# The values projection of an mLSTM layer as seven block products instead of eight

## The reference, cut to what matters

```python
proj = h @ w_in                                   # h: (tokens, 1024), after rmsnorm
q = proj[..., :HK] ...                            # HK = 4 heads x 128
k = proj[..., HK:2 * HK] ... * (MLSTM_DK ** -0.5)
v = proj[..., 2 * HK:2 * HK + HV]                 # HV = 4 heads x 256 = 1024 columns
o = proj[..., 2 * HK + HV:2 * HK + 2 * HV]        # output gate
```

## Time and profile before

| what | value |
|---|---|
| median of the timed executions | 1197.86 us (1196.89 to 1198.4, 3 runs) |
| the profiled execution, its own time | 1195.74 us |
| its span, first to last instruction | 1193.9 us |
| granted TensorE clock over the span | 0.999 of full |
| PE, DVE, ACT busy over the span | 99%, 72%, 51% |
| DMA | 148.60 MB, mean 124 GB/s |

### The profile page before, as it was taken

The page is one execution under the profiler, slowest core; times in us unless marked ns, Lnnn a source line. Parts: engine busy times, 40 slices in busy tenths (PEclk is TensorE's granted clock), DMA queues, the critical chain, the costliest instruction groups (busy, mean ns, idle before and its releaser), DMA issues.

```text
span 1193.9 us, 24091 instructions
## 1 busy us (share of the span) xinstructions
PE 1180.7 (99%) x9596; PEld 893.0 (75%) x9596; DVE 863.6 (72%) x1306; ACT 613.4 (51%) x1027; POOL 170.7 (14%) x289
## 2 busy tenths in 40 slices
PE   8999999999999999999999999999999999999998
PEld 6755777777777777777774456777777777787886
DVE  6744677587888878677774479757788888787655
ACT  6322455466555555454445469846555555544432
POOL 1000010002223223000003300000222222100001
PEclk9999999999999999999999999999999999999999
DMA  8643253235655455445546310023655456345663
GB/s 222 242 106 88 60 149 118 70 101 161 158 124 142 121 132 149 121 120 148 146 120 228 99 57 2 2 72 104 171 133 146 110 130 156 90 125 143 155 177 79
DMA packets 197626, 148.60 MB, mean 124 GB/s; under 512 B 5905, under 2 KB 178763, under 8 KB 197474
## 3 DMA queue, kind: packets, MB, share of 16 engines
q1 hardware_dynamic: 181392, 101.72, 29.5%
q0 software_dynamic: 16064, 45.68, 16.5%
q10 hardware_dynamic: 90, 0.09, 0.0%
HBM read 109.15 MB, written 9.86 MB: 100 GB/s over the span
## 4 chain that ended last, share of the span: by engine, by line
PE 88%; DVE 6%; ACT 3%; issue 1%; SPq 1%; DMA 1%; DVEq 0%
PE PS L602 36%; PE PS L824 19%; PE PS L758 16%; PE PS L618 10%; DVE P L2712 1%; DVE xT L650 1%; DVE st L2693 1%; SPq L2762 1%; PE PS L1686 1%; PE PS L1628 1%; ACT ntmp L658 1%; ACT P L2215 1%; DMA rowsF<-in_ffn_conv_b 1%; PE PS L1887 1%; ACT wH L336 0%
## 5 line engine op out<-in xcount | busy, mean ns | idle before, releaser
L824 PE MATMUL PS<-hidH,blk 128*128 128x288 f16 x1232 | 227.8, 286 | 0.0
L342 DVE SCALAR_TENSOR_TENSOR wL<-stage,wH 128x1024 f16<-128x1024 f32 x140 | 170.2, 1220 | 74.7 <-ACT wH L336 74.2
L336 ACT ACTIVATE wH<-stage 128x1024 f16<-128x1024 f32 x140 | 146.3, 1048 | 133.1 <-PE PS L618 56.7
L824 PE MATMUL PS<-hidL,blk 128*128 128x288 f16 x616 | 176.2, 286 | 0.0
L602 PE MATMUL PS<-zH,wH 128*128 128x288 f16 x832 | 170.0, 286 | 0.7 <-DVE zL L663 0.7
L602 PE MATMUL PS<-zL,wH 128*128 128x288 f16 x832 | 170.0, 286 | 0.0
L602 PE MATMUL PS<-zH,wL 128*128 128x288 f16 x832 | 170.0, 286 | 0.0
L824 PEld LDWEIGHTS PS<-hidH,blk 128*128 128x128 f16 x1232 | 120.5, 98 | 30.5 <-ACT val L547 0.3
L602 PEld LDWEIGHTS PS<-zH,wH 128*128 128x128 f16 x832 | 81.2, 98 | 22.0 <-DVE zL L663 1.3
L602 PEld LDWEIGHTS PS<-zL,wH 128*128 128x128 f16 x832 | 81.4, 98 | 20.5
L602 PEld LDWEIGHTS PS<-zH,wL 128*128 128x128 f16 x832 | 81.4, 98 | 20.5
(11 more groups left out here) (443 smaller groups left out, 2509.2 us busy)
## 6 DMA issues: line engine op xcount, KB each, us to landing
stage<-in_w_ffn_up SPq DMA_DIRECT2D x88, 512.0 KB, 4.2
quart<-in_w_ffn_down SPq DMA_DIRECT2D x32, 704.0 KB, 5.6
stage<-stage POOLq DMA_DIRECT2D x54, 256.0 KB, 4.5
stage<-in_w_mlstm_in SPq DMA_DIRECT2D x24, 512.0 KB, 4.6
stage<-in_w_swa_qkv SPq DMA_DIRECT2D x12, 512.0 KB, 4.6
quart<-quart POOLq DMA_DIRECT2D x8, 704.0 KB, 5.3
quart<-mixed POOLq DMA_DIRECT2D x8, 704.0 KB, 5.5
C<-in_state_mlstm_C POOLq DMA_DIRECT2D x4, 1024.0 KB, 7.0
```

Of the source, the lines that this page charges most:

```text
L336: nc.scalar.activation(wH[:, slot, :], stage[:, slot, :], ACT.Copy, scale=WSCALE).then_inc(hi_ready, inc)
L342: nc.vector.scalar_tensor_tensor(out=wL[:, slot, :], in0=stage[:, slot, :], scalar=WSCALE, in1=wH[:, slot, :], op0=ALU.mult, op1=ALU.subtr ...
L824: m = nc.tensor.matmul(down_bank(g), blk[:, g % RING, a, 128 * k:128 * (k + 1)], (hidH, hidL)[b][:, k, HIDDEN[j], :], start=(k == 0 and (a ...
```

## The change

The 512 prompt tokens and 1024 value columns are cut into quarters, and so are the 1024 rows of the weights. Instead of eight products of quarters there are seven (`V_A11`, `V_A12`, `V_A22`, `V_N2`, `V_S1`, `V_S3`, `V_S4`), of which some have sums of quarters on both sides. The samples' values are still plain products, made beside the four plain weight quarters; the quarter A21 is used for the samples alone. The weights are thus 16 units instead of 8.

- Four sums of quarters of x are made on DVE from `z32` in the first stage, two of them before the wait for the token factors and two behind it but ahead of the diagonal. ACT and DVE split them into halves between units of q and k.
- The right half of the value columns is loaded by SP into `v_raw`, which is the room of `C0`.
- The sums of weights: N2 is made on DVE (two subtractions); S1, S3 and S4 are made by six accumulating DMAs of 512 KB on POOL's queue, the first two after the low halves of the units of A21, the other four after N2.
- SP waits for all six sums before it loads the units of `o`.
- Partial sums: ACT evicts scaled copies of the shared products into `vM` (`keep_product`), DVE adds the others to them (`value_tile`). N2 gathers onto A11 in PSUM, and S3 onto both.
- POOL no longer waits before the cache copies, which are thus issued directly after its small loads; `load_c(0)` and `load_c(1)` move behind the low half of the last unit of S3.

```diff
-SEGS = [("qk", 8), ("v", 8), ("o", 8), ...
+SEGS = [("qk", 8), ("v", 16), ("o", 8), ...
+V_A11, V_A12, V_A21, V_A22, V_N2, V_S1, V_S3, V_S4 = range(0, 16, 2)
+        def v_high(act, n):
+            if n < V_N2:
+                act.wait_ge(v_landed, 64)
+            elif n < V_S1:
+                act.wait_ge(v_sums, 5 + n - V_N2)
+            else:
+                act.wait_ge(v_dma, 32 if n < V_S3 else 96)
+            act.wait_ge(unit_used, V0 + n - (RING - 1))
+            nc.scalar.activation(wH[:, n % RING, :], v_source(n), ACT.Copy, scale=WSCALE).then_inc(hi_ready, 1)
# PE
+            v_product(V_A11, plain(0, 0), 0, True, (0, 0))
+            v_product(V_A12, plain(KQ, 0), 2, True, (0, KQ))
+            v_product(V_A21, None, None, False, (1, 0))
+            pe.wait_ge(xs_low, 3)
+            v_product(V_A22, summed(T_4), 4, True, (1, KQ))
+            pe.wait_ge(tile_done["v"], 3)
+            gate_columns()
+            v_product(V_N2, summed(T_2), 0, False)
+            pe.wait_ge(gsem["cols"], 1)
+            keys_turn(0)
+            pe.wait_ge(free["v"], 2)
+            v_product(V_S1, summed(T_1), 2, True)
+            pe.wait_ge(tile_done["v"], 4)
+            keys_turn(1)
+            pe.wait_ge(tile_done["v"], 6)
+            pe.wait_ge(xs_low, 4)
+            v_product(V_S3, summed(T_3), 0, False)
+            keys_turn(2)
+            v_product(V_S4, plain(KQ, 2), 0, True, tile_ready=(8, 10))
+            keys_turn(3)
             keys_turn(4)
-                    pe.wait_ge(free["v"], TT + 8)
+                    pe.wait_ge(free["v"], 10)          # head_rows(0)
# ACT, the last part of the values
+            v_high(act, 12)
+            v_high(act, 13)
+            keep_product(((0, 2), (1, 3)), 0, 0, V_N2 + 2)
+            act.wait_ge(gsem["cols"], 1)
+            keys_weighted(0)
+            v_high(act, 14)
+            v_high(act, 15)
+            keys_weighted(1)
+            split_act(act, unit("o", 0, 0))
+            keep_product(((0, 0), (0, 2), (1, 1), (1, 3)), 0, 1, V_S3 + 2)
+            split_act(act, unit("o", 0, 1))
+            keys_weighted(2)
+            split_act(act, unit("o", 0, 2))
+            split_act(act, unit("o", 0, 3))
+            keys_weighted(3)
# DVE, the first stage
+            x_sum(T_1, x_quarter(0, 2), x_quarter(0, 0), ALU.subtract)
+            dve.wait_ge(v_sums, 1)
+            x_sum(T_2, t_sum[T_1], x_quarter(KQ, 2), ALU.subtract)
             dve.wait_ge(x_col, 1)
+            dve.wait_ge(v_sums, 2)
+            x_sum(T_4, x_quarter(KQ, 0), t_sum[T_2], ALU.add)
+            x_sum(T_3, x_quarter(KQ, 2), x_quarter(0, 2), ALU.subtract)
+            nc.vector.tensor_scalar(xrw[:, :], xrs[:, :], 1.0 / WSCALE, None, ALU.mult)
             for tt in range(TT):
                 m = nc.vector.tensor_scalar(diag[...], ident, xrs[:, tt:tt + 1], None, ALU.mult)
# DVE, the values
+            for n in range(4, 8):
+                v_low(dve, n)
+            dve.wait_ge(unit_used, V0 + V_A12 + 2)
+            dve.wait_ge(tile_done["v"], 2)
+            for j in range(2):
+                value_tile(j, 0, 2 + j)
+            value_n2(0)
+            value_n2(1)
+            for n in range(8, 12):
+                v_low(dve, n)
+            gate_columns()
+            v_low(dve, 12)
+            v_low(dve, 13)
...
+            split_dve(dve, unit("o", 0, 0))
+            dve.wait_ge(tile_done["v"], 10)
+            for j in range(2):
+                value_tile(2 + j, 1, 2 + j)
+            for j in range(2):
+                value_tile(j, 1, 4 + j)
+            split_dve(dve, unit("o", 0, 1))
+            split_dve(dve, unit("o", 0, 2))
+            dve.wait_ge(unit_used, V0 + V_S4 + 2)
+            dve.wait_ge(free["v"], 4)
+            for j in range(2):
+                value_tile(2 + j, 0, j)
+            split_dve(dve, unit("o", 0, 3))
# SP
+            sp.wait_ge(v_sums, 4)
+            for u in range(4):
+                sp.dma_start(v_raw[:, 1024 * u:1024 * (u + 1)]..., win[...]).then_inc(v_landed, 16)
+            sp.wait_ge(v_dma, 96)
             fm("o", win, 2 * MH * DK + MH * DV)
# POOL
-            pool.wait_ge(lo_ready, 4)
-            pool.wait_ge(nrm["lo"], TT)
-            load_c(0)
-            load_c(1)
             for name in ("k", "v"):
                 store(O["sample_" + name][0, :, 0:WIN - TB], I["cache_swa_" + name][0, :, TB:WIN])
...
+            for h in range(2):
+                pool.wait_ge(v_sums, 5 + h)
+                pool.wait_ge(lo_ready, V0 + V_A22 + h + 1)
+                pool.dma_start(v_raw[:, 1024 * (2 + h):1024 * (3 + h)], stage[:, h, :],
+                               accum_op=ALU.add).then_inc(v_dma, 16)
+                pool.dma_start(stage[:, 2 + h, :], stage[:, h, :], accum_op=ALU.add).then_inc(v_dma, 16)
+            pool.wait_ge(lo_ready, V0 + V_S3 + 2)
+            load_c(0)
+            load_c(1)
```

More of the change, by code:

```diff
@@ L1542, in keys_turn, with v_product @@
                 m.then_inc(gsem["kt"], 1)
-            for c in range(2):
-                if c:
-                    gate_columns()
-                for u in range(4):
-                    if c:
-                        keys_turn(u)
-                    num, slot, _ = unit("v", c, u)
-                    pe.wait_ge(lo_ready, num + 1)
-                    for tt in range(TT):
-                        if u == 0:
-                            pe.wait_ge(free["v"], TT * c + tt + 1)
-                        rows = ROWS[tt]
+            def v_product(n, left, bank, opens, samples=None, tile_ready=None):
+                for hu in range(2):
+                    pe.wait_ge(lo_ready, V0 + n + hu + 1)
+                    slot = (n + hu) % RING
+                    for j in range(2 if left else 0):
+                        if tile_ready and hu == 0:
+                            pe.wait_ge(tile_done["v"], tile_ready[j])
@@ L2060, in _, with keep_product, sample_values, keys_weighted @@
             nc.scalar.activation(WS[:, :], WS[:, :], ACT.Exp).then_inc(gsem["rows"], 1)
-            for u in range(4):
-                split_act(act, ahead(unit("v", 0, u)))
-            act.wait_ge(gsem["cols"], 1)
-            for j in range(4):
+            def keep_product(tiles, bank, c, used):
+                act.wait_ge(unit_used, V0 + used)
+                for j, tt in tiles:
+                    nc.scalar.activation(v_tile(tt, c), v_bank(bank + j), ACT.Copy,
+                                         scale=xrw[:, tt:tt + 1]).then_inc(tile_done["v"], 1)
+            def sample_values(c, used):
+                act.wait_ge(unit_used, V0 + used)
+                for q in range(2):
+                    m = nc.scalar.activation(vM[0:NS, 4, 2 * c + q, 0:DV], PS[NS * q:NS * (q + 1), 6 + c, 0:256],
+                                             ACT.Copy, scale=xrw[0:NS, 4:5])
+                m.then_inc(tile_done["v"], 1)
+            def keys_weighted(j):
                 act.wait_ge(gsem["kt"], j + 1)
@@ new lines, in value_tile, with value_n2 @@
+            def value_tile(tt, c, bank):
+                nc.vector.scalar_tensor_tensor(out=v_tile(tt, c), in0=v_bank(bank), scalar=xrw[:, tt:tt + 1],
+                                               in1=v_tile(tt, c), op0=ALU.mult, op1=ALU.add).then_inc(free["v"], 1)
+            def value_n2(h):
+                dve.wait_ge(v_dma, 32)
+                nc.vector.tensor_tensor(stage[:, h, :], stage[:, h, :], v_raw[:, 1024 * h:1024 * (h + 1)],
+                                        ALU.subtract).then_inc(v_sums, 1)
@@ L2774, in fm @@
                             load(unit(name, i, u), w[:, :, bass.ds(i * 512 + (c0 + 128 * u), 128)])
-            def tm(name, w, c0, chunks):
-                with sp.Fori(0, chunks) as c:
-                    for u in range(4):
-                        load(unit(name, c, u), w[:, 2 * u:2 * u + 2, bass.ds(c * 512 + c0, 512)])
             def ffn(L):
```

170 lines of the change are left out of this document (122 added, 48 removed).

## The result

| | before | after |
|---|---|---|
| median, lowest to highest (6 runs each) | 1197.92 us, 1196.89 to 1199.01 | 1203.66 us, 1202.57 to 1209.36 |
| profiled execution: time, span, mean granted clock | 1195.74, 1193.9, 0.999 | 1202.57, 1200.8, 0.996 |

The ratio after to before is 1.0058, with a 95% interval of 1.0045 to 1.0070: slower by 5.4 to 8.4 us, where 1.4 us faster was predicted, and outside the range of 1193.8 to 1201.8.

The account below looks back on a forecast made before the run. PE, busy 99% of the span, was taken as the bound. Won 5.4 us, lost 1.7 + 0.6 + 1.7 = 4.0, net -1.4: 1197.9 - 1.4 = 1196.5 us, range 1193.8 to 1201.8.

Parts of the forecast that it names:

- The matmuls: In the values, eight products of 24 matmuls become seven; with saved changes of shape, 5.4 us won.
- The sums of x: First stage: four sums on DVE delay the diagonal and unit 2's low half; 1.7 us lost (1.2 to 2.1).
- The accumulating DMAs: Four 512 KB transfers for S3 and S4 land 11.6 us after first issue; cost zero, cover 1.3 us.
- The sum: Whole kernel: won 5.4, lost 1.7 + 0.6 + 1.7 = 4.0, net -1.4 us.
- The fourth product: At S4, PE waits for ACT to keep two results from bank 0; 0.6 us lost (0.3 to 1.0).
- The end of the values: At head_rows(0), the last two value tiles stand behind o's low halves on DVE; 1.7 us lost (1.0 to 7.2).
- The clock: Rival: TensorE's clock falls in the new waits; with 5 us of work behind them 1201.5; chance 0.02.
- the slower side of the wait at the end of the values: Rival at head_rows(0): o2 lands 13.9 us after issue, tail costs 7.2 us, time 1202.0; chance 0.12.
- the slow side: Whole kernel: chance 0.22 of a time over 1200.3 us, from 0.12 + 0.05 + 0.03 + 0.02 of the rivals.
- Everything behind the values shifts with PE: After the values, all later work moves with PE, which stays the bound; no further loss priced.
- The range: Whole kernel: 1193.8, with the least of the three waits, to 1201.8, with o2 nearly as late as in the slow rival.
- the least of the three waits: Lower bounds of the losses: 1.2 us in the first stage, 0.3 at S4, 1.0 at head_rows(0).

Follow-up runs that it names:

- the kernels with three and five edits: Changed kernel, memories' loads late, value tiles before o splits, x sums behind diagonal: 1197.28 us; plus third product's own sums, o0 split behind kept product and tiles: 1194.82 us.
- kernel before with nine memsets: Kernel before plus nine memsets into dead buffers on VectorE ahead of the third value tile of the second half: 1202.44 us, ratio 1.0041.

## Why the prediction was wrong

Its steps, in its order:

- **The matmuls** (won 5.4): right. The values' lengths in the kernels with three and five edits come out as -5.4 and their waits, to 0.1 us.
- **The sums of x** (lost 1.7): right in kind and size, 1.8 of the 2.16; the other 0.4 lie ahead of the first transposes of `rowsF`. Four sums of 1.22 and a wait of 1.25 at the diagonal are as forecast. That the sums could stand behind the diagonal at no cost I hadn't looked for.
- **The accumulating DMAs** (cost zero, cover 1.3): the size was off. The second group's last transfer landed 13.75 us after the first issue, not 11.6: the bulk moved from 90.8 to 101.2 at some 200 GB/s, as estimated, and then 2 us passed with the engines 7% busy until the last of the four was in (512 KB each, issued at 89.48 to 92.97). The sum had no term for such a tail. With ScalarE's two splits and two kept tiles (1.27 us, not the 1.1 assumed) behind it, the cover of 1.3 became a wait of 1.84.
- **The fourth product** (0.6): 1.01, as a kept tile takes 0.61, and both in bank 0 had to be done.
- **The end of the values** (1.7): 2.89. The place and the mechanism were right, an `o` load behind the memories holding two value tiles in VectorE's queue. It came later because the sums before it did, and the load took 8.85 us (8.1 in the prediction).
- **The clock** (a rival with 0.02, priced at 0 in the sum): this is the step that failed by most; the cover of the accumulating DMAs, 1.84 us, is the next. I read from the earlier trace rows that 1.68 of 2 us idle left the clock at 1.00, and called the new waits "of that size"; the wait was 2.89 and cost another 3.04. The one row wasn't enough for that size either, as the fall behind 1.39 us at the entry shows. The kernel before with a wait of 2.94 shows it by itself. The rival had the right mechanism but 5 us for it, not 3.04; that its 1201.5 comes near 1203.7 is luck, as the waits were too short in its sum by another 3.9. I had given the slower side of the wait at the end of the values up to 7.2 us, without joining the clock's price to any wait above 2 us. With that, the slow side gets more than its 0.22. The prediction did name the sign: a wait of PE of over 2 us in any one place would make the sum wrong.
- **Everything behind the values shifts with PE**: wrong by 1.03 us in the profile after, in the first feed-forward layer, for a cause that stays open.
- **The range**: its lower end, 1193.8, doesn't follow from "the least of the three waits"; with 1.2, 0.3 and 1.0 the sum is 1195.0, as the forecast's own bounds have it.

Errors all of one sign: 0.5 + 1.84 + 0.4 + 1.2 + 3.0 + 1.0 = 8.0, against a miss of 8.3 us in the profiled execution (1202.57 for 1194.3) and 7.2 in the median.

The Trainium skill, "TensorE: Matmul & The Clock Gate", section "What's actually happening", has two levels of the clock and a fall after idleness. The profiles agree. In and just behind the values the clock is at 1.00 behind waits of 0.5, 0.6, 1.0, 1.2, 1.7 and 1.84 us, and at 0.50 behind 2.89, 2.90, 2.94 and 4.42 us. At the entry it is at 1.00 behind 1.30, 1.53, 1.68 and 1.75 us and at 0.50 behind 1.39, 1.98 and 2.43 us. So the length of one wait doesn't decide it alone, and what else does stays open.

## What to carry to other kernels

Where TensorE is the bound, price a wait at its length only while it is short: the shortest behind which the clock fell here was 1.39 us, the longest behind which it stayed 1.84. A single wait of nearly 3 us cost twice its length or more in the three profiles that have one, so the largest of several waits is the one to take apart first. When transfers or loads come later, look in each engine's queue for what stands behind the instruction that waits for them and doesn't need them: moving two value tiles and the last weighted keys ahead of the splits of `o` was worth 6.3 us by the ratios (5.3 by the landmarks), about the 5.4 of the saved matmuls. The gain of an edit can be hidden by a fall of the clock behind it, so combine edits before one is thrown away.

## What the runs showed of the hardware beyond that

- At the entry, the fall of the clock came 1.3 and 2.1 us after TensorE had begun again (0.6 behind the wait of 2.43 us), and lasted 3.4, 3.4 and 6.8 us. Behind the waits of 2.9 us the granted clock fell only 0.9 to 1.5 us after TensorE had begun to work again (behind the one of 4.42 us it fell before that), and it stayed at its 1.2 GHz level for 6.8 us (changed kernel, kernel before with nine memsets, and the wait of 4.42 us) or 10.2 us (sums behind the diagonal), with TensorE busy all the time once it had begun again.
- The accumulating DMAs between buffers on chip moved some 200 GB/s, with one of 256 KB under way (197 to 217) as with four of 512 KB (184 to 229), and the last landing came 2 us behind the bulk: two of 512 KB landed after 6.6 and 8.0 us, four after 4.6, 7.2, 10.1 and 12.1.
- With the buffers moved by 20 bytes, copies out of them were slower: 4.7 and 7.0 us instead of 4.4 and 6.8 for 864 KB. The Trainium skill, "DMA: Bandwidth & Descriptors", section "How a descriptor splits into AXI transactions", says that a piece which doesn't start on a boundary of 256 bytes costs additional beats. Whether that is the cause is not shown: no run tells where the pieces start in either kernel. The time of the changed kernel didn't move with it (0.9980 against 0.9978); that of the kernel before was 1.4 us longer (0.4 to 2.5), hardly clear of noise.
